# A hybrid decoder trunk on one core: weight unit 0 split in two halves, three warming products fewer, and the states of heads 0 and 1 woven with projection tiles

## The reference

```python
h = _rmsnorm(x, ln_mix)                                  # 320 x 1024
proj = einsum('bld,de->ble', h, w_in)                    # 1024 x 4104
rq, rk, rv, rg, mq, mk, mv, mo, mi, mf = _split(proj, AB_SPLITS)
# retention, 4 heads of 128 (chunked over the prompt; S carried for the samples)
intra = einsum('bhts,bhsv->bhtv', einsum('bhtk,bhsk->bhts', qc, kc) * decay, vc)
inter = einsum('bhtk,bhkv->bhtv', qc, S) * q_dec
S_new = S * chunk_dec + einsum('bhsk,bhsv->bhkv', kc * k_dec, vc)
# mLSTM, 4 heads: causal conv and silu on mq, mk; gates mi, mf; state C, n, m
```

## Time and profile before

| | us |
|---|---|
| median of 3 runs | 1504.23 |
| lowest, highest | 1499.2, 1638.78 |
| profiled execution, its own time | 1500.16 |
| its span | 1498.4 |
| TensorE busy | 1472.0 (98%) |
| VectorE, ScalarE, GpSimd busy | 1152.9, 935.0, 87.3 |

### The profile page before, as it was taken

One profiled execution on the slowest core, in us unless ns is written; L12 is line 12 of the kernel. 1 busy time (PEld: TensorE's weight loads), 2 busy tenths in 40 slices (PEclk: granted clock), 3 DMA queues, 4 the chain that ended last, 5 costly groups with the idle time before them and its releaser, 6 DMA issues.

```text
span 1498.4 us, 22988 instructions
## 1 busy us (share of the span) xinstructions
PE 1472.0 (98%) x8445; PEld 1305.7 (87%) x8445; DVE 1152.9 (77%) x1307; ACT 935.0 (62%) x973; POOL 87.3 (6%) x96
## 2 busy tenths in 40 slices
PE   9999999999999989999999999999999999999997
PEld 8899899999999979989788888888888888888885
DVE  5756678545455697776798888988889888898887
ACT  5434555343333764354777878778787787877875
POOL 1023110000000000120300000000000000000011
PEclk9999999999999999999999999999999999999999
DMA  9577725997445523441999999999999999999994
GB/s 252 132 126 141 151 81 149 285 294 208 128 141 177 159 86 128 145 146 61 372 408 387 391 363 393 379 381 391 362 390 382 382 391 359 395 379 382 398 341 167
DMA packets 213588, 404.04 MB, mean 270 GB/s; under 512 B 13471, under 2 KB 130491, under 8 KB 213390
## 3 DMA queue, kind: packets, MB, share of 16 engines
q1 hardware_dynamic: 202976, 372.82, 71.4%
q0 software_dynamic: 6320, 22.20, 4.9%
q10 hardware_dynamic: 4222, 8.06, 1.4%
HBM read 372.75 MB, written 30.28 MB: 269 GB/s over the span
## 4 chain that ended last, share of the span: by engine, by line
PE 89%; DVE 7%; ACT 2%; issue 1%; DMA 1%; POOL 0%; ACTq 0%; DVEq 0%; POOLq 0%
PE bank L510 26%; PE bank L512 26%; PE bank L511 26%; PE bank L739 1%; PE bank L1170 1%; DVE dense_lo L1904 1%; PE bank L781 1%; PE bank L684 1%; PE bank L994 1%; ACT dense_hi L1395 0%; PE bank L731 0%; PE bank L1107 0%; DVE arena L2044 0%; PE bank L1097 0%; PE bank L692 0%
## 5 line engine op out<-in xcount | busy, mean ns | idle before, releaser
L2403 DVE TENSOR_TENSOR w_lo<-arena,w_hi 128x2048 fp32r<-128x2048 f32 (+1 forms) x280 | 597.0, 2166 | 81.2 <-ACT w_hi L1742 80.2
L1742 ACT ACTIVATE w_hi<-arena 128x2048 fp32r<-128x2048 f32 (+1 forms) x280 | 501.8, 1820 | 115.0 <-PE bank L512 111.7
L510 PE MATMUL bank<-w_hi,xg_hi 128*128 128x512 f32 x704 | 275.6, 391 | 0.5 <-DVE w_lo L2403 0.3
L512 PE MATMUL bank<-w_hi,xg_lo 128*128 128x512 f32 x704 | 274.1, 389 | 0.0
L511 PE MATMUL bank<-w_lo,xg_hi 128*128 128x512 f32 x704 | 274.0, 389 | 0.0
L1904 DVE TENSOR_TENSOR dense_lo<-ring,dense_hi 128x2048 fp32r<-128x2048 f32 (+1 forms) x77 | 165.5, 2150 | 122.3 <-ACT dense_hi L1395 122.1
L1395 ACT ACTIVATE dense_hi<-ring 128x2048 fp32r<-128x2048 f32 (+1 forms) x78 | 140.5, 1802 | 139.3 <-PE bank L512 119.0
L510 PEld LDWEIGHTS bank<-w_hi,xg_hi 128*128 128x128 f32 x704 | 132.2, 188 | 30.7 <-issue 3.1
L512 PEld LDWEIGHTS bank<-w_hi,xg_lo 128*128 128x128 f32 x704 | 132.1, 188 | 27.7
L511 PEld LDWEIGHTS bank<-w_lo,xg_hi 128*128 128x128 f32 x704 | 132.2, 188 | 26.9
L510 PE MATMUL bank<-h_hi,dense_hi 128*128 128x320 f32 x448 | 142.2, 318 | 1.6 <-DVE h_lo_a L1974 1.1
(11 more groups left out here) (461 smaller groups left out, 2378.0 us busy)
## 6 DMA issues: line engine op xcount, KB each, us to landing
arena<-in_w_moe_down SPq DMA_DIRECT2D x176, 512.0 KB, 6.6
arena<-in_w_moe_gate SPq DMA_DIRECT2D x128, 512.0 KB, 7.3
arena<-in_w_moe_up SPq DMA_DIRECT2D x128, 512.0 KB, 7.2
arena<-in_w_moe_gate SPq DMA_DIRECT2D x64, 384.0 KB, 4.2
arena<-in_w_moe_up SPq DMA_DIRECT2D x64, 384.0 KB, 5.3
ring<-in_w_in_ab SPq DMA_DIRECT2D x32, 512.0 KB, 8.8
ring<-in_w_in_c SPq DMA_DIRECT2D x32, 512.0 KB, 4.7
expert_rows<-ZERO SPq DMA_DIRECT2D x12, 1024.0 KB, 7.6
```

Of the source, the lines that this page charges most:

```text
L510: mm(out, left[0], right[0], start=start, stop=False)
L512: return mm(out, left[1], right[0], start=False, stop=stop)
L1742: fn(WH[SLOT_OF[p]][:, 0:unit_size(p)], STAGE[:, s, 0:unit_size(p)], ACT.Copy).then_inc(S("unit_hi"), 1)
L2403: v.tensor_tensor(WL[w][:, 0:n], STAGE[:, s, 0:n], WH[w][:, 0:n].bitcast(F32), ALU.subtract).then_inc(S("unit_split"), 1)
```

## The change

1. **Halves of unit 0.** The first of its two transfers counts on a semaphore of its own, `first_half_landed`. ScalarE makes the high part of that half right behind the token roots, ahead of the copy of the parameters, and the other half behind it. VectorE makes the low part in two halves as well. `landed(n)` gives the count that the other waiters expect, since buffer 0 now has one count of 16 less.
2. **WARM = 15** instead of 18.
3. **Order of words.** `mq3 state0 wh wl wh state1 ... mk0 mk1` becomes `mq3 along state0 wh wl wh mk0 along state1 ... mk1`.
4. Semaphores are merged: `history_zero` into `zero` (its count is 4 now), `lb_max` and `lb_exp` into one.

```diff
-    silu0 mq3 state0 wh wl wh state1 conv2 wl score2 conv3 silu1 mk0 mk1 silu2 wh silu3 score3 weigh2 mk2
+    silu0 mq3 along state0 wh wl wh mk0 along state1 conv2 wl score2 conv3 silu1 mk1 silu2 wh silu3 score3 weigh2 mk2
@@
-        WARM = 18
+        WARM = 15
@@
+        def landed(n):
+
+            return 32 * (n // DSTAGE + 1) - (16 if n % DSTAGE == 0 else 0)
@@
-            pe.wait_ge(S("zero"), 3)
+            pe.wait_ge(S("zero"), 4)
@@ sync, load_dense
-                        sp.dma_start(v[:, k - 4 * half:k - 4 * half + 2, :], src).then_inc(sem, 16)
+                        first = n == 0 and k == 0
+                        sp.dma_start(v[:, k - 4 * half:k - 4 * half + 2, :], src).then_inc(
+                            S("first_half_landed") if first else sem, 16)
@@ scalar
             fn(RS[:, :], RS[:, :], ACT.Sqrt, scale=1.0 / D, bias=C("eps")).then_inc(S("token_roots"), 1)
+            first, lead = next(split), slice(0, UNIT // 2)
+            act.wait_ge(S("first_half_landed"), 16)
+            fn(unit_flat(first, DWH)[:, lead], unit_flat(first, DST)[:, lead], ACT.Copy).then_inc(S("first_half_hi"), 1)
             free(fn(prm[:, :], take("prm")[:, 0:NPRM], ACT.Copy))
+            act.wait_ge(dense_landed[0], landed(0))
+            rest = slice(UNIT // 2, UNIT)
+            fn(unit_flat(first, DWH)[:, rest], unit_flat(first, DST)[:, rest], ACT.Copy).then_inc(S("dense_hi"), 1)
@@
-            split_dense()
             for k in range(KD // 2):
                 first_high(k)
@@ vector
-            split_dense()
+            first = next(split)
+            for at, ready in ((slice(0, UNIT // 2), "first_half_hi"), (slice(UNIT // 2, UNIT), "dense_hi")):
+                dve.wait_ge(S(ready), 1)
+                ins = v.tensor_tensor(unit_flat(first, DWL)[:, at], unit_flat(first, DST)[:, at],
+                                      unit_flat(first, DWH)[:, at].bitcast(F32), ALU.subtract)
+            ins.then_inc(S("dense_split"), 1)
```

More of the change, by code:

```diff
@@ L1280, in _ @@
                 if 0 <= piece < NZERO:
-                    sp.wait_ge(S("zero"), 3)
+                    sp.wait_ge(S("zero"), 4)
                     flat = XD[CAP:(NBLOCK + 1) * CAP, :].rearrange("(p b) (r d) -> p (b r) d", p=P, d=256)
@@ L1391, in split_dense @@
                     return
-                act.wait_ge(dense_landed[n % DSTAGE], 32 * (n // DSTAGE + 1))
+                act.wait_ge(dense_landed[n % DSTAGE], landed(n))
                 if n >= DSPLIT:
@@ L1417, in _ @@
             act.wait_ge(S("scales_one"), 1)
-            act.wait_ge(S("zero"), 3)
+            act.wait_ge(S("zero"), 4)
             fn(V1[:, :], ZERO[:, 0:3], ACT.Sqrt)
@@ L1568, in _ @@
                     b = take("carry")
-                    act.wait_ge(S("history_zero"), 1)
+                    act.wait_ge(S("zero"), 4)
                     fn(CARRY.rearrange("p k n -> p (k n)"), b[:, 0:192], ACT.Copy)
@@ L1623, in _ @@
             act.dma_start(O["mn_p"][0, 0], NTO[32:36, :]).then_inc(S("stores"), 16)
-            act.wait_ge(S("lb_max"), 1)
-            fn(LBT[:, 0:2, :], LBT[:, 0:2, :], ACT.Exp).then_inc(S("lb_exp"), 1)
+            act.wait_ge(S("lower_bound"), 1)
+            fn(LBT[:, 0:2, :], LBT[:, 0:2, :], ACT.Exp).then_inc(S("lower_bound"), 1)
             projected_out("oab", "n1", U_F, HH_F)
@@ L2218, in _ @@
             v.tensor_tensor(LBT[:, 0, :], bound[:, 0, :], LBT[:, 2, :], ALU.subtract)
-            v.tensor_tensor(LBT[:, 1, :], bound[:, 1, :], LBT[:, 2, :], ALU.subtract).then_inc(S("lb_max"), 1)
-            dve.wait_ge(S("lb_exp"), 1)
+            v.tensor_tensor(LBT[:, 1, :], bound[:, 1, :], LBT[:, 2, :], ALU.subtract).then_inc(S("lower_bound"), 1)
+            dve.wait_ge(S("lower_bound"), 2)
             step(v.tensor_tensor(LBT[:, 2, :], LBT[:, 0, :], LBT[:, 1, :], ALU.add))
@@ L2599, in _ @@
             g = nc.gpsimd
-            g.memset(XC[:, :, 0:3], 0.0).then_inc(S("history_zero"), 1)
+            g.memset(XC[:, :, 0:3], 0.0).then_inc(S("zero"), 1)
             g.memset(ZERO[:, :], 0.0).then_inc(S("zero"), 1)
@@ L2630, in spread @@
                 g.tensor_tensor(VX[0:SMP], v1, m, ALU.mult).then_inc(S(f"vx{layer}"), 1)
-            pool.wait_ge(dense_landed[0], 32)
+            pool.wait_ge(dense_landed[0], landed(0))
             pool.dma_start(wgate[:, :, :], w_ab[:, :, 4096:4104]).then_inc(S("wgate_in"), 16)
@@ L2654, in conv_tail @@
                 g.tensor_copy(CT[:, k, 3:27].rearrange("p (b t) -> p b t", t=3), tail).then_inc(S("conv_tail"), 1)
-            pool.wait_ge(S("history_zero"), 1)
+            pool.wait_ge(S("zero"), 4)
             for name, u in AB_STEPS:
```

## The result

The changed kernel takes **1523.93 us** (median, 1522.58 to 1528.71); the kernel before beside it took 1501.72. The ratio is 1.0153, 95% interval 1.013 to 1.0176, and leaves out one slow run of the kernel before, of 1638.78. That is slower by some 23 us, clear of the noise though under 2%, where 3.5 were forecast. The profiled executions show nearly all of it: span 1520.8 against 1498.4.

What follows compares the result with a forecast made beforehand. TensorE's own products were taken as the bound, busy 1472.0 of 1498.4 us. Opening -1.8 and heads +5.3 gave +3.5 on the profiled 1500.16: 1503.7, with 8 in 10 within 1498 to 1509.

Steps and rivals of the forecast that it cites:

- Opening, -1.8: Before the first real product: halves of unit 0 and fewer warming products bring it to 14.14, a gain of 1.8 us.
- The gap of 5.2 us before the key tile: Heads 0 and 1: TensorE idles from 96.65 to 101.85, waiting for unit 8's split and VectorE's low part.
- I take the middle, 1.5 a head, ends 1.14 and 2.0: Heads 0 and 1: sample products woven into a tile take 1.5 us a head, against 1.14 back to back.
- the 0.9 of the text: Heads 0 and 1: the loss of 5.3 us moves by 0.9 less or more with weaving at its ends.
- the upper end: Weaving at heads 0 and 1: 2.0 us a head, 0.5 more than taken, if changing the tiling mode drains TensorE.
- I price that as the slow stretch of before, 1.6 us: Restart at the key tile: low clock costs 1.6 us, 1.06 in scores and 0.5 in the tile.
- slow for as long as the opening's ramp: End for the clock behind the gap: slow as in the opening's thirty records of 9.13 us, 0.9 us more loss.
- rival 1: Gap before the key tile, with a clock that stays high or soon recovers: +3.7 - 1.8, so 1502; chance 0.17.
- The stores and loads of the states move past one copy of the carried rows; none is asked for before the next heads: State transfers at the heads: reordering past that copy was given no cost in the sum.
- Rivals: Gap with high clock, 1502, chance 0.17; opening gives half, 1504.6, chance 0.12; key tile hardly waits, 1497, chance 0.11.
- The forecast's sign: Whole kernel: slower, by +3.5 us, since the loss at heads 0 and 1 exceeds the opening's gain.

Runs made afterwards that it cites:

- experiment 7: The opening taken apart: changed kernel with old order of words and WARM = 18, 1499.73 us; kernel before with only WARM = 15, 1501.34 us.
- experiment 8: Experiment 5's woven kernel, sample products of two heads on 128 rows zeros, 32 rows zeros, 128 rows key data, their sample states left out: 1511.77, 1514.09, 1513.28 us.
- experiment 4: Experiment 2's kernel with 12 zero products put into the gap ahead of the key tile: 1507.04 us, ratio 1.0031 to the kernel before.
- experiment 1: Each part alone: changed kernel with the old order of words, 1497.59 us; kernel before with the new order of words, 1524.42 us.
- experiment 2: Changed kernel with the load of head 3's states issued right behind the store of head 0's, ahead of the waiting copy: 1512.45 us, ratio 1.0076.
- experiment 3: Changed kernel with the first key tile in one piece and head 1's state behind it: 1508.97 us, ratio 1.0047.
- experiment 5: Changed kernel with `wh wl` (unit 8's split) moved ahead of `mq3`: both tiles woven, 1511.66 us; both tiles whole, 1503.72 us.
- experiment 9: Changed kernel with the old order of words, except head 0's samples woven into the last query tile: 1503.82 us, ratio 1.0012.
- the opening's: Changed kernel with the old order of words, so halves of unit 0 and 15 warming products without weaving: 1497.59 us, ratio 0.9981.

## Why the prediction was wrong

- **Opening, -1.8: right.** Measured -1.88, step for step (half at 10.03, product at 14.08, forecast 14.14). The part of it ascribed to fewer warming products was not theirs (experiment 7).
- **The gap of 5.2 us before the key tile: right.** 5.11 measured, put down to VectorE's low part as forecast, and ScalarE's split at 97.45 (forecast 97.5 in positions of before, which the opening should have made 95.7: the 1.8 between is the weaving's extra cost, which had already gone in ahead of it). The gap came out in size because both its ends moved by the same 1.8.
- **Weaving, "I take the middle, 1.5 a head, ends 1.14 and 2.0": failed as a size, 3.6 us in two heads.** A woven head costs 3.29 us at the full clock, outside both ends (which make 0.7 less and 1.0 more in two heads, not the 0.9 of the text). I built the upper end from a 256-column product and "a little" for a change of shape; a 32-row piece costs 0.39 us more than a 128-row one in the same place (1.26 less 0.87, experiment 8), and 0.54 more than in a row of its own kind. The Trainium skill's rule that a change of tiling mode drains TensorE (TensorEngine Tiling, "Key Properties") spoke for the upper end, and the trace agrees with its direction; if the drain is what those 0.39 us are, it is larger than I gave it.
- **"I price that as the slow stretch of before, 1.6 us": the step that failed in the first half.** The key tile lost 5.4 us to the clock (12.36 against 6.91 in experiment 4). The stretch of before was ended by plain token products; in a tile with four 32-row pieces among its products the clock stayed at 0.50 to its end. Three executions with the gap and the woven tile (the changed kernel, experiments 1 and 2) show 12.36 us each, and three with whole tiles behind a gap (3, 5, 9) are back in about 4 us. Even my end, "slow for as long as the opening's ramp", allowed 0.9 more. The 1.6 was itself 0.4 too much, 1.2 by experiment 1: I took the first score product's extra time behind the 32-row ones for the clock. And it was a fall that three other executions of the same order (experiments 1 and 7) do not have, so that it couldn't count as evidence against rival 1, as I used it; that the clock did fall behind 5.1 us is shown four times (the changed kernel, experiments 1, 2 and 3).
- **"The stores and loads of the states move past one copy of the carried rows; none is asked for before the next heads": the step that failed in the second half, and the largest.** I counted the instruction as passed and did not ask what it waits for. It waits for a tile that the change itself moved behind a gap and a slow clock. That gave 3.7 us of gap and 7.6 of slow products: 9.8 us of the spans, and all 11.3 by positions, come back when the load goes ahead (experiment 2).
- **Rivals.** None had a second gap. The forecast's sign held. The sum with what was measured is -1.9 for the opening, 4.5 of idle time, 4.3 of weaving, 3.9 of clock and 11.3 behind: +22 instead of +3.5. Opening and first gap alone make +2.6, so the sign was right for the reason given.

**Open:** why the clock sometimes falls with no gap in front, or only a short one. Woven tiles did it twice in one execution (experiment 5) and not, for the first such tile, in the changed kernel nor in experiments 1, 2, 4, 8 and 9; the 0.62 us before head 1's samples did it in the kernel before and in none of the three others with that order. Behind a gap, tiles with thin pieces of either kind (32 rows, or 8 columns) were at 0.50 for 10 us and more, but no run had full 128 x 256 pieces there, so it is open whether thin pieces do it or any weaving.

## What to carry to other kernels

When a step moves past an instruction on a queue, follow that instruction's own wait to its source: if it waits for work that the change delays, everything queued behind it is delayed too, transfers with long landings first. Price a gap of the matmul engine with what stands behind it: plain full products bring the clock back in a few microseconds, tiles with thin pieces woven in did not here. And 32-row pieces are cheap only in a row.

## What the runs showed of the hardware

- A 32-row fp32 pair of 256 columns costs 0.28 us in a row (eight records in 1.14), 0.82 among 128-row products at the full clock; the same piece on 128 rows costs 0.43 there.
- Behind an idle gap of 1.9 to 5.1 us the clock was back in about 4 us with whole tiles (experiments 3, 5 and 9). With 32-row pieces woven in it took 12.4 (the changed kernel, experiments 1 and 2), with 8-column ones 10.5 to 18 (the second gap, and experiments 1, 5 and 8; the longest two have a run of 32-row products behind the woven tile). Filled with zero products, the gap of 5 us left it at 1.00 (experiment 4).
- One kernel's executions can lie 18 us apart (1500.93 to 1518.64 in experiment 5); the kernel before spread over 14 beside the last three runs (1498.62 to 1512.76). One profile of such a kernel is one of its courses. The part behind the retention states, the same in all, took 1369.4 to 1372.5 us in the profiled executions, so spans alone don't place an edit worth 1 or 2 us; positions do.
- The load of 512 KB of states landed 11.0 us behind its issue in the changed kernel, 10.0 in experiment 2, 8.6 in the opening's and 5.0 in experiment 3: it moves by 6.0 us, more than either gap of the changed kernel.
